# S5 scan of an encoder trunk: real and imaginary parts laid side by side in columns instead of on the two halves of the partitions

## The reference, cut to what matters

```python
for d in range(2):                                    # forward, backward
    lam_bar = jnp.exp(lam * dt)
    b_bar = ((lam_bar - 1.0) / lam)[..., None] * b_mat
    bu = jnp.einsum('bsgc,gpc->sbgp', ug, b_bar)       # 16 groups, 64 complex states
    _, states = lax.associative_scan(_linear_combine, (a, bu), axis=0, reverse=(d == 1))
    y = y + jnp.real(jnp.einsum('sbgp,gcp->bsgc', states, c_mat)).reshape(B, S, S5_WIDTH)
z = jax.nn.gelu(y)
out = z * jax.nn.sigmoid(z @ w_glu + b_glu)
```

## Time and profile before

| | us |
|---|---|
| median of 3 runs | 1585.46 (1584.69 to 1585.79) |
| the profiled execution, its own time | 1585.26 |
| its span in the profile | 1583.4 |
| PE busy | 1530.6 (97%) |
| DVE busy | 621.3 (39%) |
| ACT busy | 425.2 (27%) |
| POOL busy | 377.4 (24%) |

### The profile page before, as it was taken

How to read it: one execution, slowest core, us unless ns; L and a number is a source line. 1 busy time by engine, 2 the same in 40 slices (tenths; PEclk the granted TensorE clock), 3 DMA queues, 4 the chain that set the end, 5 groups by cost and what they waited for, 6 DMA issues and landing times.

```text
span 1583.4 us, 20219 instructions
## 1 busy us (share of the span) xinstructions
PE 1530.6 (97%) x8156; PEld 785.9 (50%) x8156; DVE 621.3 (39%) x1244; ACT 425.2 (27%) x762; POOL 377.4 (24%) x432
## 2 busy tenths in 40 slices
PE   8999999999999999998999999999999999999986
PEld 4655566555444444443347546655554444444432
DVE  2697546462122212311427965474522122123114
ACT  3654641211111111111235547403111111111102
POOL 4671790000000000000265637600000000000003
PEclk9999999999999999999999999999999999999999
DMA  9300403959999999999950003059699999999997
GB/s 394 145 0 14 147 1 89 426 220 424 427 426 428 426 428 426 428 425 429 363 247 1 1 29 132 1 175 409 240 426 427 425 427 426 428 427 428 427 426 305
DMA packets 58546, 470.02 MB, mean 297 GB/s; under 512 B 19481, under 2 KB 19609, under 8 KB 30258
## 3 DMA queue, kind: packets, MB, share of 16 engines
q1 hardware_dynamic: 51202, 452.37, 68.9%
q0 software_dynamic: 7104, 16.24, 2.7%
q10 hardware_dynamic: 144, 0.07, 0.0%
HBM read 447.69 MB, written 26.74 MB: 300 GB/s over the span
## 4 chain that ended last, share of the span: by engine, by line
PE 82%; DMA 9%; DVE 6%; ACT 2%; issue 1%; POOL 0%; SPq 0%; POOLq 0%; DVEq 0%; ACTq 0%
PE bank L1029 24%; PE bank L1068 12%; PE bank L670 10%; PE bank L1019 9%; PE bank L801 7%; DMA ring<-wu 5%; DMA ring<-wd 2%; PE bank L745 2%; PE bank L732 2%; PE bank L662 2%; PE bank L762 2%; PE bank L1006 1%; PE bank L1053 1%; PE bank L656 1%; PE bank L878 1%
## 5 line engine op out<-in xcount | busy, mean ns | idle before, releaser
L2266 POOL DMA_INDIRECT expert_rows<-raw_qd,store_rows x60 | 58.8, 980 | 1002.5 <-ACT raw_qd L1470 944.3
L1029 PE MATMUL bank<-ring,hbuf 128*64 128x512 f32 x640 | 281.2, 593 | 6.8 <-DMA ring<-wu 6.8
L1030 PE MATMUL bank<-ring,hbuf 128*64 128x512 f32 x640 | 281.4, 593 | 0.0
L2018 DVE COPY raw_qd<-bank 128x256 f32<-128x256 f32 x64 | 27.2, 424 | 642.0 <-PE bank L1053 642.0
L670 PE MATMUL bank<-hbuf,ring 128*128 128x512 f32 x480 | 210.1, 595 | 0.6 <-DVE hbuf L1533 0.6
L1029 PEld LDWEIGHTS bank<-ring,hbuf 128*64 128x64 f32 x640 | 86.8, 137 | 185.4 <-issue 185.1
L1029 PE MATMUL bank<-raw_qd,hbuf 128*64 128x512 f32 x372 | 163.7, 592 | 3.6 <-DMA hbuf<-wu 3.6
L1068 PE MATMUL bank<-ring,raw_qd 128*64 128x512 f32 x352 | 160.4, 598 | 5.7 <-DVE raw_qd L2018 3.1
L1070 PE MATMUL bank<-ring,raw_qd 128*64 128x512 f32 x352 | 160.5, 598 | 0.0
L1019 PE MATMUL bank<-raw_qd,x 128*128 128x192 f32 x896 | 159.5, 332 | 0.0
L1463 ACT ACTIVATE raw_qd<-bank 64x512 f32<-64x512 f32 x64 | 37.8, 590 | 416.7 <-PE bank L1030 416.7
(11 more groups left out here) (401 smaller groups left out, 2247.2 us busy)
## 6 DMA issues: line engine op xcount, KB each, us to landing
ring<-wg SPq DMA_DIRECT2D x38, 2048.0 KB, 19.2
ring<-wd SPq DMA_DIRECT2D x38, 2048.0 KB, 19.8
ring<-wu SPq DMA_DIRECT2D x34, 2048.0 KB, 22.2
ninth_slot<-wd SPq DMA_DIRECT2D x20, 2048.0 KB, 20.2
raw_qd<-wg SPq DMA_DIRECT2D x18, 2048.0 KB, 19.7
hbuf<-wu SPq DMA_DIRECT2D x18, 2048.0 KB, 23.3
ring<-w_in SPq DMA_DIRECT2D x6, 2048.0 KB, 19.4
raw_qd<-wg SPq DMA_DIRECT2D x6, 1792.0 KB, 12.5
```

What stands on the lines that cost most here:

```text
L1029: mm(pb[2 + par][0:CAP, :], tokens[:, k, :], gates[k], start=(k == 0), stop=(k == KT - 1))
L1030: last = mm(pb[2 + par][CAP:P, :], tokens[:, k, :], ups[k], start=(k == 0), stop=(k == KT - 1))
L2266: G.indirect_dma_start(out=half_rows, out_offset=bass.IndirectOffsetOnAxis(ap=store_i[:, e:e + 1], axis=0), in_=y_sb[e % 2], in_offset=Non ...
```

## The change

The parts now lie in columns, and two groups lie on the two halves of the partitions: group g (0 to 7) on 0 to 63 and group g + 8 on 64 to 127, columns 0 to 255 of a quarter real and 256 to 511 imaginary. A quarter is 4 such pairs of one direction.
- `chunk_inputs(q)` is 16 products of 64 weight columns each instead of 8 of 128, written to the half of the output partitions that belongs to the group. All four quarters follow each other.
- Both half-swap products are gone (`sine_parts` and the loop at L899), and the matrix `half_swap` and the column `sign` leave the constants. `MIXER_AT` goes from column 320 to 319 and `EARLY_UP` from 2048 to 1920.
- DVE reads the other part by reversed columns (`[:, ::-1]`). `scanned` now has two half-size operations in place of L1754 and a second full product (`turned_by_sine`); `states(q)` is 4 operations on 64 partitions each and writes `S5` in its old layout.
- The tables hold 16 pairs instead of 32, so each table operation of POOL has half the elements. POOL brings the angles and `rho` into pairs by small copies (`by_pairs`).
- `early(2)` to `early(5)` stand between the chunk inputs and the S5 outputs, 6 and 7 under gelu. `first_finals` takes the place of `final(0)` and `final(1)`: both groups' tile 6, then both groups' tile 7.

```diff
-        X_BANK = [(pb[4], pb[5]), (pb[0], pb[1]), (pb[2], pb[3]), (pb[4], pb[5])]
+        X_BANK = (pb[4], pb[0], pb[2], pb[3])
...
-                for i in range(8):
-                    dg = 8 * q + i
-                    u = U5[:, dg % G5, :] if dg < G5 else U5[:, dg % G5, ::-1]
-                    last = mm(X_BANK[q][0][:, NK * i:NK * i + NK], Bt[:, dg, :], u, start=True, stop=True)
+                for part in range(2):
+                    for i in range(4):
+                        for half in range(2):
+                            g = 4 * (q % 2) + i + G5 // 2 * half
+                            u = U5[:, g, :] if q < 2 else U5[:, g, ::-1]
+                            at = NK * (4 * part + i)
+                            last = mm(X_BANK[q][HD * half:HD * half + HD, at:at + NK],
+                                      Bt[:, G5 * (q // 2) + g, HD * part:HD * part + HD], u, start=True, stop=True)
                 last.then_inc(s["xin"], 1)
...
             for q in range(4):
-                pe.wait_ge(s["z"], on("z") + max(q + 1, 2 + q // 2))
-                mm(pb[q][:, :], cst("half_swap"), flat(T2[:, 8 * q:8 * q + 8, :]),
-                   start=True, stop=True).then_inc(s["zs"], 1)
-            early(4)
+                chunk_inputs(q)
+            for n in range(2, 6):
+                early(n)
...
-            early(5)
             early(6)
+            early(7)
...
-            early(7)
-            pe.wait_ge(s["o_c"], on("o_c") + 2)
+
+            def first_finals():
+                for k in range(6, KT):
+                    pe.wait_ge(s["o_c"], on("o_c") + k - 5)
+                    for n in range(2):
+                        if n == 1 and k == 6:
+                            pe.wait_ge(s["gx"], on("gx") + 4)
+                        last = mm(pb[n][:, :], mixed[k][:, 0:P], w_o[n][:, k, :], start=(k == 6), stop=(k == KT - 1))
+                        if k == KT - 1:
+                            last.then_inc(s["wo"], 1)
...
             def rotated(q):
-                r = slice(8 * q, 8 * q + 8)
                 dve.wait_ge(s["xin"], on("xin") + q + 1)
-                a = X_BANK[q][0][:, :].rearrange("p (d k) -> p d k", d=8)
-                TT(T2[:, r, :], a, sinT[:, r, :], ALU.mult).then_inc(s["xr"], 1)
-                TT(T1[:, r, :], a, cosT[:, r, :], ALU.mult).then_inc(s["xr"], 1)
+                a = X_BANK[q][:, :].rearrange("p (r j k) -> p r j k", r=2, j=4)
+                TT(T2[q], a[:, ::-1], both_parts(sinT, q), ALU.mult)
+                TT(T1[q], a, both_parts(cosT, q), ALU.mult).then_inc(s["xr"], 1)
...
-                link(TT(T1[:, r, :], T1[:, r, :], X_BANK[q][1][:, :].rearrange("p (d k) -> p d k", d=8), ALU.subtract))
+                TT(T1[q][:, RE], T1[q][:, RE], T2[q][:, RE], ALU.add)
+                link(TT(T1[q][:, IM], T1[q][:, IM], T2[q][:, IM], ALU.subtract))
...
-                link(TT(T1[:, r, :], T2[:, r, :], cosT[:, r, :], ALU.mult))
+                TT(turned_by_sine[q], T2[q][:, ::-1], both_parts(sinT, q), ALU.mult)
+                link(TT(T1[q], T2[q], both_parts(cosT, q), ALU.mult))
+
+            def states(q):
+                for half in range(2):
+                    h = slice(HD * half, HD * half + HD)
+                    g = G5 * (q // 2) + 4 * (q % 2) + G5 // 2 * half
+                    for part, op in ((RE, ALU.subtract), (IM, ALU.add)):
+                        rows = S5[HD * part:HD * part + HD, g:g + 4, :]
+                        ins = TT(rows[:, :, 1:NK] if q < 2 else rows[:, :, NK - 2::-1], T1[q][h, part, :, 0:NK - 1],
+                                 turned_by_sine[q][h, part, :, 0:NK - 1], op)
+                return ins
...
-            tm = raw[:, 5120:6144].rearrange("p (d k) -> p d k", d=DG)
-            tm_last = ring[:, 1, 1026:2050].rearrange("p (d k) -> p d k", d=DG)
+            tm = raw[:, 5120:5632].rearrange("p (j k) -> p j k", j=G5)
+            tm_last = ring[:, 1, 1026:1538].rearrange("p (j k) -> p j k", j=G5)
...
-            link(G.tensor_copy(rho, pv_rho8[:, :, None].broadcast_to([P, DG, NK])))
+            rho_pairs = Wi[:, 0, 0:G5]
+            pool.wait_ge(s["bc"], on("bc") + 3)
+            by_pairs(rho_pairs, pv_rho8)
```

More of the change, by code:

```diff
@@ L76 @@
     ("ident", P), ("chunk_end", NMORE), ("over_id", NOVER), ("slot_rank", NE), ("half_row", NE), ("slot_id", CAP),
-    ("is_re", 1), ("is_im", 1), ("sign", 1), ("eps", 1), ("one", NE),
-    ("mask_f", P), ("mask_b", P), ("head_ones", P), ("half_swap", P), ("cos", T), ("sin", T), ("chunk_on", T),
+    ("is_re", 1), ("is_im", 1), ("eps", 1), ("one", NE),
+    ("mask_f", P), ("mask_b", P), ("head_ones", P), ("cos", T), ("sin", T), ("chunk_on", T),
     ("before", P), ("ones", P), ("fold", RW), ("group_id", EG), ("expert_id", NE), ("odd", NE)])
@@ L290, in trunk @@
             bt_v="DVE: even banks of Bt evacuated",
-            xin="PE: S5 chunk inputs of a quarter", xr="DVE: sine, cosine parts of a quarter", xw="PE: sine parts with halves swapped",
+            xin="PE: S5 chunk inputs of a quarter", xr="DVE: sine and cosine parts of a quarter",
             z="DVE: S5 quarters scanned",
-            zs="PE: S5 states swapped", xs="DVE: S5 states", y5="PE: S5 outputs", y5_e="ACT: S5 outputs, first half",
+            xs="DVE: S5 states", y5="PE: S5 outputs", y5_e="ACT: S5 outputs, first half",
             y5_v="DVE: S5 outputs, second half", yt="PE: S5 outputs feature-major", ge="DVE: gelu argument", gx="ACT: gelu, then GLU tanh", z5="DVE: gelu",
@@ L374, in weights @@
             return ring[:, i, 0:8 * width].rearrange("p (k c) -> p k c", k=KT)
-        SPLIT, EARLY_UP = 6 * FF, 4 * FF
+        SPLIT, EARLY_UP = 6 * FF, CONST["before"][0] - MIXER_AT
         w_o = [ring[:, 4 + i, :].rearrange("p (k c) -> p k c", k=KT) for i in range(2)]
@@ L961, in router @@
                 last.then_inc(s["rlT"], 1)
-            final(0)
-            final(1)
+            first_finals()
             final(2)
@@ L1768, in vector_program @@
             scanned(0)
+            V.memset(S5[:, 0:G5, 0], 0.0)
+            V.memset(S5[:, G5:DG, NK - 1], 0.0)
+            states(0)
             rotated(2)
@@ L1771, in vector_program @@
             early(2)
+            states(1)
             rotated(3)
             scanned(2)
+            states(2)
             early(3)
             scanned(3)
-            V.memset(S5[:, 0:G5, 0], 0.0)
-            V.memset(S5[:, G5:DG, NK - 1], 0.0)
-            for q in range(4):
-                r = slice(8 * q, 8 * q + 8)
-                dve.wait_ge(s["zs"], on("zs") + q + 1)
-                link(TT(T2[:, r, :], pb[q][:, :].rearrange("p (d k) -> p d k", d=8), sinT[:, r, :], ALU.mult))
-                to = S5[:, r, 1:NK] if q < 2 else S5[:, r, NK - 2::-1]
-                ins = TT(to, T1[:, r, 0:NK - 1], T2[:, r, 0:NK - 1], ALU.subtract)
-            ins.then_inc(s["xs"], 1)
+            states(3).then_inc(s["xs"], 1)
             early(4)
@@ L1789, in vector_program @@
                           pb[5][:, :].rearrange("p (g t c) -> p g t c", g=4, t=SC)).then_inc(s["y5_v"], 1)
+            early(5)
             dve.wait_ge(s["yt"], on("yt") + 1)
@@ L2258, in pool_program @@
             pool.wait_ge(s["ho"], on("ho") + 2)
-            link(G.tensor_copy(rho, pv_rho8[:, :, None].broadcast_to([P, DG, NK])))
+            rho_pairs = Wi[:, 0, 0:G5]
+            pool.wait_ge(s["bc"], on("bc") + 3)
+            by_pairs(rho_pairs, pv_rho8)
+            rho_parts = rho.rearrange("p (q r j) k -> p q r j k", q=4, r=2)
+            for part in range(2):
+                ins = G.tensor_copy(rho_parts[:, :, part], rho_pairs.rearrange("p (q j) -> p q j", q=4)[:, :, :, None]
+                                    .broadcast_to([P, 4, 4, NK]))
+            link(ins)
             G.memset(rho[:, :, 0], 0.0).then_inc(s["bc"], 1)
@@ L2355, in constants @@
     put("head_ones", (p // HD) == (q // HD))
-    put("half_swap", p == (q + HD) % P)
     put("before", p < q)
@@ L2380, in constants @@
     put("is_im", p >= HD)
-    put("sign", np.where(p < HD, 1.0, -1.0))
     put("eps", EPS)
```

58 lines of the change are left out of this document (25 added, 33 removed).

## The result

| | us |
|---|---|
| changed kernel, median of 7 runs | 1578.24 (1575.25 to 1581.04) |
| kernel before, 7 runs beside it | 1586.39 (1584.69 to 1588.57) |
| ratio, 95% interval | 0.9947 (0.9935 to 0.996) |
| the profiled execution, its own time and span | 1579.17, 1577.3 |

The change makes the kernel faster by 8.2 us. The forecast was 15.4 us; 1578.24 lies just above the upper end of its range. The sign is right, about half of the size is missing.

What follows compares the result with a forecast made beforehand. PE's chain ahead of the router was taken to bound the kernel, with the weights' stream following it. Per layer -6.9 + 0.2 + 0.2 - 1.2 = -7.7 us, -15.4 in all, gave 1570.0 us, range 1567.3 to 1577.3.

Steps and rivals of the forecast that it cites:

- Half-swap products, -6.9 us: S5 on PE: eight products of 512 columns go, lying wholly on the path, saving 6.9 us per layer.
- Chunk inputs, +0.2 us: S5 on PE: 128 passes of 64 weight columns at 56 ns take 7.2 us instead of 7.0 per layer.
- the bounds are 6.5 and 8.7 us: S5 chunk inputs: the 128 passes take between 6.5 and 8.7 us, from rows at 51 and 68 ns.
- The low end of my range: Chunk inputs at 6.5 us help little, since states at 267.0 bind: 0.9 + 0.1 us per layer better, 1568.
- No wait is added: S5: DVE keeps up with PE at early(5) and the outputs, with margins of only 0.2 and 0.9 us.
- The states: S5 on DVE: state operations at 0.31 us each, done at 267.0, before the outputs start at 267.9.
- The tail, +0.2 us: From S5 outputs to first finals: missing cover of early(7) costs some 0.2 us per layer.
- HGRN, -1.2 us: HGRN: POOL's shorter table operations free DVE, so PE's wait near 120 us goes, saving 1.2 us per layer.
- The stream follows: Behind the router: each us gained ahead moves the weights' stream and layer's end by one; opposing rival 1579.7, chance 0.04.
- The rival of the eleventh slot: Experts' weight loads: writes from column 319 at half speed would cost 17 us, giving 1587.2; chance 0.03.
- that of the 64-column products: S5 chunk inputs: 64-column products cost as 128-column ones, 14.1 us instead of 7.2, giving 1583.7; chance 0.04.
- The first rival: S5: DVE becomes the bound, state operations at 0.60 us, outputs 3.7 us late, giving 1577.3; chance 0.13.

Runs made afterwards that it cites:

- e_fill3: Changed kernel plus three unread products of 512 columns ahead of early(5) to fill PE's wait; 1573.09 us, 0.9916 of the kernel before.
- e_early3: Changed kernel with DVE adding early group 3 ahead of the scan of quarter 2; 1575.54 us, 0.9929 of the kernel before.
- e_align: Changed kernel with one constants column put back, so the eleventh slot's weights begin at column 320 again; 1576.97 us, 0.9942 of the kernel before.
- the second one: Second profile of the changed kernel, unaltered, in another launch; 1574.61 us, 0.9927 of the kernel before.
- c_before: The kernel before, unaltered, run again for a second profile; 1586.58 us.

## Why the prediction was right and wrong

**Half-swap products, -6.9 us.** They are gone as forecast. No run isolates their price.

**Chunk inputs, +0.2 us: wrong.** The size was read from rows with 128 moving columns (56 ns) and bounded from below by rows that come in one half at a time (51 ns). Measured: 31 ns a pass, 4.4 us with the wait inside. The step "the bounds are 6.5 and 8.7 us" failed: its low end was the cheapest row of the trace, and I wrote it down as if nothing could be cheaper. By itself the error is in the kernel's favour. The low end of my range had an error of its own: with 6.5 us for the chunk inputs I let the states (267.0) bind, but `early(5)` then still waits for the addition at 262.5, and the outputs start at 267.65, 0.2 us earlier and not 0.9.

**"No wait is added": wrong, and this is the step that decided.** DVE's part of it was right within 0.5 us (262.94 against 262.5), though two errors cancel: the second rotation starts 1.0 us earlier than assumed (242.56, not 243.6), and twelve state operations at 0.43 instead of 0.31 take 1.4 us more. PE's part rested on the 7.2 us. With 4.4 us PE comes 2.9 us early. I had a price for a late DVE, and none for an early PE: I took idle time of PE ahead of a fixed event as free. It is not, since the granted clock falls behind it. That costs 1.6 us in layer 0 and 1.7 in layer 1 of the first profile (56.78 and 56.87 against 55.17), 3.3 of the 5.0 us that S5 lacks. `e_fill3` shows it: same start of `early(5)`, no loss of clock, time 1573.1. The other 0.8 us a layer are still missing in `e_fill3`: its S5 outputs start 0.4 us late, since DVE's addition does, and its tail is 0.3 too long.

**The states: 0.9 us late.** 267.93 against 267.0: sixteen state operations at 0.43 (1.9 us more) less the earlier start (1.0). In `e_fill3` they do not bind. In `e_early3` they do: PE idles 2.9 us for them.

**The tail, +0.2 us: 0.3 too low.** From the start of the GLU products to the end of the first finals it takes 7.4 us (287.49 to 294.89) where the working had 7.1 (285.6 to 292.7). The four products of `first_finals` start 3.77 us behind the GLU products instead of 3.6, and take 3.63 us instead of 3.43.

**HGRN, -1.2 us: right in its mechanism and, in layer 0, in its size** (-1.10). In layer 1 the idle of 1.18 us is gone too, but the stretch up to S5 gains only 0.43 us. Two waits in attention are new there (0.23 us ahead of an L756, 0.24 ahead of the next L732), and from start to start the two places take 0.58 us more than before.

**The stream follows: right.** See the 454 us above. The rival of the eleventh slot is refuted by `e_align`, that of the 64-column products by 31 ns a pass. The first rival had the right place and sign, DVE as the bound in S5 and 1577.3 us. But its mechanism is not what happened: the state operations cost 0.43, not 0.60, and the outputs (270.0 instead of 267.9) were late mostly through the clock of `early(5)`. That its number came so near is luck.

**The sum.** 15.4 forecast, 8.2 and 11.6 in two launches. S5 lacks 5.0 us of it in the first profile (3.3 by the clock), 6.4 in the second one (4.7 by the clock: 58.17 and 56.87 against 55.17). HGRN in layer 1 lacks 0.8. The late start, the stream's 1.9 us and the 0.6 behind the router belong to the first profile's execution. The observable named beforehand ("it is wrong if `early(5)` waits for DVE by more than 1 us") is the one that came true.

## What to carry to other kernels

When a step gets cheaper than assumed, follow who arrives early, and where; a wait of PE for a fixed event may cost more than its length, so price what runs behind it too. Before moving work of the slower engine, look for the tie: here two alternating banks, not DVE's amount of work, and four more banks were free. A term that a bound says is "at least 6.5 us" deserves the question which row would be the cheapest conceivable, not which is nearest.

## What the runs showed of the hardware

- Idle of 2.5 to 2.95 us on PE was followed in 11 of 14 cases by a stretch at half the granted clock (1.2 instead of 2.4 GHz; passes of L897 every 0.107 us instead of 0.054), and 3 times by none. A shorter idle can do it: that of 1.15 to 1.18 us in HGRN of the kernel before was followed by such a stretch in one of four places (layer 1 of `c_before`). Idle of 0.83 to 0.89 us, which all profiles have ahead of the transposition, never was. A stretch at half clock does not follow from the length of one idle alone, then, and what else decides these runs do not show.
- A pass with 64 weight columns and 64 moving columns takes 31 ns when the halves alternate and 40 ns in runs of four; with 128 weight columns it took 110 (32 passes in 3.52 us). The Trainium skill, TensorE: Matmul & The Clock Gate, section LDWEIGHTS (loading the stationary operand), has the load cost its columns divided by 1.2 in ns. For 128 columns the trace agrees (107 ns by the page). For 64 an estimate from the page is 53: the 51 ns of the earlier trace rows agree with it, the 31 and the 40 ns do not.
- DVE operations on 64 partitions with 252 columns, as `states(q)` has them, follow at 0.43 us, those on 128 partitions with 256 columns at 0.34 (262.85 to 263.19). The first kind lasts 0.39 us and the next begins only behind its end; of the second kind the next begins before the 0.42 us of the first are over. Whether it is the output, which changes between the halves of the partitions, or the pattern of 4 x 63 columns, no run tests.
- POOL's table products hold DVE up about in proportion to their number: with six more its last HGRN scan ends 2.8 us later, with twelve 6.0; with six more, DVE's product L1583 takes 1.45 us instead of 0.69. The Trainium skill, SBUF — State Buffer, section SBUF: two separate sides, says that a DVE operation with two SBUF inputs and a GpSimd operation exclude each other for their whole length; by that rule DVE loses time with each of POOL's operations and not only with long ones, and the runs with six and twelve more agree (2.8 and 6.0 us).
